# A hybrid HGRN and Hyena layer with a gated FFN on one core: half of the output projection under the spectral products, the other half token tile by token tile into the FFN

## What is computed

```python
def _mixer(h, rows, s0, l, p):
    proj = jnp.einsum('bld,de->ble', h, p['w_in'][l])          # 4096 columns
    q, ff, fb, iv, g, hy = jnp.split(proj, cuts, axis=-1)
    ...                                                        # HGRN: chunked scans, 4 heads of 128
    o = o * lax.rsqrt(jnp.mean(o * o, axis=-1, keepdims=True) + EPS)
    o_hg = o.reshape(B, L, HG_WIDTH) * jax.nn.silu(g.astype(F32))
    hyc = _dwconv3(hy, p['hy_conv_w'][l], rows).astype(F32)
    v, x1, x2 = jnp.split(hyc, [HY_WIDTH, 2 * HY_WIDTH], axis=-1)
    u = x1 * v
    z = _long_conv(u, kern) + p['hy_d'][l].astype(F32) * u
    y_hy = x2 * z
    y_hy = y_hy * lax.rsqrt(jnp.mean(y_hy * y_hy, axis=-1, keepdims=True) + EPS) * p['hy_norm_w'][l]
    merged = jnp.concatenate([o_hg, y_hy], axis=-1)
    return jnp.einsum('ble,ed->bld', merged, p['w_out'][l])

def _layer(x, cvec, rows, s0, l, p):
    ...
    x = x + g1 * mix
    h = _rmsnorm(x, p['norm2_w'][l]) * (1 + sc2) + sh2
    x = x + g2 * _convffn(h, rows, l, p)   # up 1024 -> 5632, conv, silu(gate) * val, down 2816 -> 1024
```

## Time and profile before

| what | value |
|---|---|
| median of 3 runs | 1025.52 us (1025.45 to 1026.12) |
| profiled execution, its own time | 1025.82 us |
| its span | 1024.0 us |
| busy share of the span | PE 92%, PE weight loads 81%, DVE 62%, ACT 32%, POOL 1% |
| chain that ended last | PE 81%, DVE 12%, ACT 3%, DMA 2% |
| mean granted clock of PE | 0.971 of full speed |

### The profile page before, as it was taken

How to read it: one execution, slowest core, us unless ns; L and a number is a source line. 1 busy time by engine, 2 the same in 40 slices (tenths; PEclk the granted TensorE clock), 3 DMA queues, 4 the chain that set the end, 5 groups by cost and what they waited for, 6 DMA issues and landing times.

```text
span 1024.0 us, 13691 instructions
## 1 busy us (share of the span) xinstructions
PE 944.6 (92%) x5564; PEld 825.9 (81%) x5564; DVE 639.3 (62%) x825; ACT 330.5 (32%) x571; POOL 14.6 (1%) x24
## 2 busy tenths in 40 slices
PE   6789999999999999549797999999999999999996
PEld 1247988989899889238676999988999998899985
DVE  4874357687586775886548666643666664466655
ACT  2462432342433422104116333321233331133332
POOL 0000000000000000000100000000000000000000
PEclk9899999999999999869997999999999999999998
DMA  8544234323432333021511222222122222222102
GB/s 298 189 166 162 79 127 144 89 83 124 149 117 67 111 125 98 0 103 41 185 42 62 83 83 72 74 83 83 62 83 71 74 81 86 74 71 70 55 1 103
DMA packets 26711, 99.06 MB, mean 97 GB/s; under 512 B 3256, under 2 KB 3640, under 8 KB 26009
## 3 DMA queue, kind: packets, MB, share of 16 engines
q1 hardware_dynamic: 24728, 89.06, 26.0%
q0 software_dynamic: 1920, 9.13, 2.7%
HBM read 95.01 MB, written 3.16 MB: 96 GB/s over the span
## 4 chain that ended last, share of the span: by engine, by line
PE 81%; DVE 12%; ACT 3%; DMA 2%; issue 2%; POOL 0%; SPq 0%; ACTq 0%; DVEq 0%
PE ps L1197 23%; PE ps L1199 22%; PE ps L1198 22%; PE ps L1375 3%; PE ps L1215 2%; DVE h_lo L817 1%; PE ps L1491 1%; PE ps L1234 1%; DMA x<-in_x_prompt 1%; DMA raw<-in_slots 1%; DVE h_hi L816 1%; PE ps L1387 1%; PE ps L1225 1%; PE ps L1464 1%; PE ps L1395 0%
## 5 line engine op out<-in xcount | busy, mean ns | idle before, releaser
L1197 PE MATMUL ps<-h_hi,w_hi 128*128 128x320 f32 x1152 | 360.4, 313 | 0.1
L1199 PE MATMUL ps<-h_hi,w_lo 128*128 128x320 f32 x1152 | 355.9, 309 | 0.0
L1198 PE MATMUL ps<-h_lo,w_hi 128*128 128x320 f32 x1152 | 355.8, 309 | 0.0
L1197 PEld LDWEIGHTS ps<-h_hi,w_hi 128*128 128x128 f32 x1152 | 216.4, 188 | 2.2 <-ACT KK L689 0.8
L1198 PEld LDWEIGHTS ps<-h_lo,w_hi 128*128 128x128 f32 x1152 | 216.4, 188 | 0.1
L1199 PEld LDWEIGHTS ps<-h_hi,w_lo 128*128 128x128 f32 x1152 | 216.2, 188 | 0.0
L809 DVE TENSOR_TENSOR w_lo<-raw,w_hi 128x1024 fp32r<-128x1024 f32 x106 | 129.3, 1225 | 128.4 <-ACT w_hi L548 123.7
L548 ACT ACTIVATE w_hi<-raw 128x1024 fp32r<-128x1024 f32 x106 | 111.1, 1052 | 134.4 <-PE ps L1199 126.2
L1197 PE MATMUL ps<-w_hi,a_hi 128*128 128x512 f32 x220 | 86.7, 394 | 0.0
L1199 PE MATMUL ps<-w_hi,a_lo 128*128 128x512 f32 x220 | 86.3, 392 | 0.0
L1198 PE MATMUL ps<-w_lo,a_hi 128*128 128x512 f32 x220 | 85.4, 388 | 0.0
(11 more groups left out here) (249 smaller groups left out, 1081.6 us busy)
## 6 DMA issues: line engine op xcount, KB each, us to landing
raw<-in_slots SPq DMA_DIRECT2D x154, 512.0 KB, 3.8
xin<-in_x_sample SPq DMA_DIRECT2D x4, 512.0 KB, 6.0
grow<-gates POOLq DMA_DIRECT2D x1, 2048.0 KB, 7.2
x<-in_x_sample POOLq DMA_DIRECT2D x4, 512.0 KB, 6.4
out_y_sample<-x SPq DMA_DIRECT2D x4, 512.0 KB, 2.6
decay<-in_decay SPq DMA_DIRECT2D x1, 1280.0 KB, 10.7
ktab<-in_ktab SPq DMA_DIRECT2D x1, 1024.0 KB, 5.8
utab<-in_utab POOLq DMA_DIRECT2D x1, 1024.0 KB, 6.3
```

The lines of the kernel that those rows point to most:

```text
L1197: mm(out, lhs[0], rhs[0], start=first, stop=False)
L1198: mm(out, lhs[0], rhs[1], start=False, stop=False)
L1199: return mm(out, lhs[1], rhs[0], start=False, stop=last)
```

## The change

1. In the projection the order of a head's tiles becomes q, ff, fb, Hyena, Hyena, g, the x2 tiles of Hyena come last, and the head steps begin with half 7 instead of 9. ACT's `ada_row` goes ahead of the wait for the half. The first three units of the output projection are split during the last tiles.
2. The heads' outputs are split between the two joins of the u spectrum. PE multiplies the HGRN half of the output projection (both column halves, 10 results) right after the forward transforms; ACT copies the results raw to `x1`.
3. The Hyena row norm no longer scales y ahead of the product: y times its weight is split per 128 channels as soon as it is there (`split_y`), the sums over channels are made token-major as five columns, and the reciprocal root of 128x5 scales the result rows in `mix_tile`, which also adds the HGRN half, the gate and the residual. The inverse tables use the memory of the forward ones, and residual rows and gates are loaded after the spectral products.
4. PE multiplies the second half tile by tile (`mix`), turns each tile (`turn_tile`) as soon as it is normed, and the FFN begins with the first halves of three up tiles, which need token tiles 0 to 2 only (`ffn_halves`); tiles 3 and 4 are turned between them.
5. The FFN's splits stand `LEAD_FFN` = 4 units ahead and behind the work of the unit, instead of 3 and ahead of it.

The diff's core:

```diff
-    for _kind in ("q", "hy", "ff", "fb", "hy", "g"):
+    TILES += [("q", _g), ("ff", _g), ("fb", _g), ("hy", HY_TILES[2 * _g]), ("hy", HY_TILES[2 * _g + 1]), ("g", _g)]
-FIRST_STEP = 9
+FIRST_STEP = 7
+LEAD_FFN = 4
+def ffn_halves(r):
+    units = range(2 * ROUNDS[r][1])
+    first = 3 if r == 0 else 0
+    return [(u, half) for half in range(2) for u in units[:first]] + [(u, half) for u in units[first:] for half in range(2)]
...
 # ACT, projection loop
                 for unit in ahead(n):
                     split_hi(unit)
+                if n in ADA_TURN:
+                    ada_row(ADA_TURN[n])
                 eng.wait_ge(sem("half_made"), n + 1)
...
-                if n in ADA_TURN:
-                    ada_row(ADA_TURN[n])
...
 # ACT, the HGRN half and the tiles
+            for n in range(2):
+                for i in range(NT):
+                    eng.wait_ge(sem("hg_mixed"), n * NT + i + 1)
+                    A(x1[:, n, i, :], ps[:, HG_BANKS[(n * NT + i) % 2], :], ACT.Copy).then_inc(sem("raw_taken"), 1)
+                for k in range(2):
+                    split_hi(UNIT_WOUT + 4 + 2 * n + k)
+            def scale_tile(i):
+                eng.wait_ge(sem("norm_used"), i + 1)
+                A(xn[:, i % 2, :].rearrange("p (n c) -> p n c", c=HW), x1[:, :, i, :], ACT.Copy,
+                  scale=stat[:, 1, 1, i:i + 1]).then_inc(sem("xn_ready"), 1)
+            def modulate_tile(i):
+                for k in range(KD):
+                    last = A(hf2[:, i % 2, k * P:(k + 1) * P], ps[:, TURN_BANKS[i] + k // 4, k % 4 * P:(k % 4 + 1) * P],
+                             ACT.Identity, scale=gain[:, 1, k, s:s + 1], bias=mod[:, 3 * KD + k, s:s + 1])
+            norm_tile(0)
+            scale_tile(0)
+            norm_tile(1)
+            scale_tile(1)
+            modulate_tile(0)
+            norm_tile(2)
+            scale_tile(2)
+            modulate_tile(1)
+            modulate_tile(2)
+            split_hi(UNIT_FFN)
+            norm_tile(3)
+            scale_tile(3)
+            split_hi(UNIT_FFN + 1)
+            modulate_tile(3)
+            norm_tile(4)
+            scale_tile(4)
+            split_hi(UNIT_FFN + 2)
+            modulate_tile(4)
+            split_hi(UNIT_FFN + 3)
...
 # DVE
+            join_u(0)
+            eng.wait_ge(sem("half_made"), NH)
+            link(V.tensor_copy(h_hi[:, 0:NC, :], o_hg[:, :, :]))
+            link(V.tensor_tensor(h_lo[:, 0:NC, :], o_hg[:, :, :], h_hi[:, 0:NC, :].bitcast(F32), ALU.subtract), "heads_split")
+            join_u(1)
+            split_lo(UNIT_WOUT + LEAD)
+            multiply(0)
+            multiply(1)
+            for k in range(2):
+                split_lo(UNIT_WOUT + 4 + k)
...
+            def mix_tile(i):
+                link(V.scalar_tensor_tensor(out=x, in0=ap(ps, MIX_BANKS[i] * 512, row), scalar=rhy[:, 2, i:i + 1],
+                                            in1=x, op0=ALU.mult, op1=ALU.add), "mixed_taken")
+                link(V.tensor_tensor(x, x, ap(grow1, s * D, row), ALU.mult))
+                link(V.tensor_tensor(x, x, ap(xres, i * D, row), ALU.add), "x1_ready")
+            def norm_row(i):
+                eng.wait_ge(sem("norm_ready"), NT + i + 1)
+                link(V.reciprocal(stat[:, 1, 1, i:i + 1], stat[:, 1, 1, i:i + 1]), "norm_used")
+            mix_tile(0)
+            norm_row(0)
+            mix_tile(1)
+            norm_row(1)
+            mix_tile(2)
+            split_tile(0)
+            norm_row(2)
+            mix_tile(3)
+            split_tile(1)
+            split_tile(2)
+            split_lo(UNIT_FFN)
+            norm_row(3)
+            mix_tile(4)
+            split_lo(UNIT_FFN + 1)
+            split_tile(3)
+            norm_row(4)
+            split_lo(UNIT_FFN + 2)
+            split_tile(4)
+            split_lo(UNIT_FFN + 3)
...
                 for n in range(2):
                     for k in range(nf // 2):
-                        split_lo(unit + LEAD)
+                        split_lo(unit + LEAD_FFN)
                         unit += 1
                     for i in range(NT):
                         eng.wait_ge(sem("down_made"), (2 * r + n) * NT + i + 1)
...
 # PE
+            for n in range(2):
+                units = [unit_ready(UNIT_WOUT + 2 * n + p) for p in range(2)]
+                for i in range(NT):
+                    ...
+                    last.then_inc(sem("hg_mixed"), 1)
...
+            mix(0)
+            mix(1)
+            mix(2)
+            turn_tile(0)
+            eng.wait_ge(sem("ysum_ready"), 1)
+            mix(3)
+            turn_tile(1)
+            turn_tile(2)
+            eng.wait_ge(sem("h_full"), KD + 1)
+            mix(4)
+            def before_half(n):
+                at = n - NH
+                if at >= 3:
+                    eng.wait_ge(sem("half_free"), n - 2)
+                if at in (0, 3):
+                    eng.wait_ge(sem("h_split"), KD + (3, 5)[at // 3])
+                if at == 1:
+                    turn_tile(3)
+                    eng.wait_ge(sem("mixed_taken"), 4)
+                if at == 2:
+                    turn_tile(4)
```

More of the change, by code:

```diff
@@ L171, in stream @@
                 out += [("ada", e, 2 * j), ("ada", e, 2 * j + 1)]
-    return out + [("weight", n) for n in range(UNIT_WOUT, NU)]
+    return out + [("weight", n) for n in range(UNIT_WOUT + LEAD, NU)]
 STREAM = stream()
@@ new lines, in _ @@
+                for u, half in ffn_halves(r):
+                    f, gv = divmod(u, 2)
+                    t = t0 + f
+                    eng.wait_ge(sem("half_made"), n + 1)
+                    if t >= 2 and half == 0:
+                        eng.wait_ge(sem("fconv"), 2 * (t - 2) + gv + 1)
+                    spread(ps[:, half_bank(n), 0:HT], padf[:, t % 2, gv, :], half, "half_free")
+                    n += 1
+                    if half and gv == 0:
+                        eng.wait_ge(sem("fconv"), 2 * t + 1)
+                        A(cf[:, 0, :], cf[:, 0, :], ACT.Silu).then_inc(sem("silu_done"), 1)
+                    elif half:
+                        eng.wait_ge(sem("act_ready"), t + 1)
+                        if r and f == 0:
+                            eng.wait_ge(sem("down_made"), 2 * r * NT)
+                        A(a_hi[:, f, :], actf[:, :], ACT.Copy).then_inc(sem("ahi_ready"), 1)
+                    if half:
+                        split_hi(unit + LEAD_FFN)
+                        unit += 1
@@ L1417, in half_product, with turn_u @@
                 last.then_inc(sem("half_made"), 1)
+            def turn_u(i):
+                for c in range(NC):
+                    if i < 4:
+                        e, k = divmod(i, 2)
+                        src = ap(u_hy, c * T + 2 * P * k + e, [(2, P)])
+                    else:
+                        src = u_hy[:, c, TS:T]
+                    last = nc.tensor.transpose(ps[:, U_BANKS[i], c * P:(c + 1) * P], src, ident[:, :])
+                last.then_inc(sem("u_turned"), 1)
             for n in range(NH):
@@ L1474, in sum_channels @@
             def sum_channels(c):
                 eng.wait_ge(sem("ysq_ready"), c + 1)
[L1476 to L1478 removed]
+                for i in range(NT):
+                    last = mm(ps[:, SUMS, c * NT + i:c * NT + i + 1], sq[:, i * P:(i + 1) * P], ones[:, 0:1],
+                              start=True, stop=True)
@@ L1517, in _, with mix @@
-            turn(xn, 1, (), lambda k: None)
+            units = [unit_ready(UNIT_WOUT + 4 + p) for p in range(4)]
+            def mix(i):
+                order = [(n, k) for k in range(NC, KD) for n in range(2)]
+                if i:
+                    order.sort()
+                for n, k in order:
+                    if i == 0 and n == 0:
+                        eng.wait_ge(sem("y_split"), k - NC + 1)
+                    last = split_product(ps[:, MIX_BANKS[i] + n, :], [x[:, k, i * P:(i + 1) * P] for x in (h_hi, h_lo)],
+                                         [w[:, k % 2 * HW:(k % 2 + 1) * HW] for w in units[2 * n + (k - NC) // 2]],
+                                         k == NC, k == KD - 1)
+                    if i == NT - 1 and k == KD - 1:
+                        last.then_inc(sem("wout_used"), 1)
+                    elif k == KD - 1 and n == 1:
+                        last.then_inc(sem("mixed"), 1)
+                    if i == 0 and k == KD - 1 and n == 0:
+                        sum_channels(NC - 1)
@@ L1528, in _ @@
+                unit += 2 * nf
                 for half in range(2):
```

515 lines of the change are left out of this document (249 added, 266 removed).

## The result

| | before | changed |
|---|---|---|
| median | 1025.82 us (1025.45 to 1028.58, 4 runs) | 992.90 us (990.59 to 994.55, 4 runs) |
| profiled execution | 1025.82 us, span 1024.0 | 991.46 us, span 989.7 |
| ratio | | 0.9672 (0.9642 to 0.9701) |
| busy share of PE, DVE, ACT | 92%, 62%, 32% | 95%, 64%, 35% |

The change is faster, but 992.9 us lies above the range of 974 to 992; of the 43.5 us forecast, 34.4 came between the two profiled executions and 32.9 between the medians. To find the missing 9.2 us I cut both profiled executions at four marks that PE's rows give: the first product of the projection, the end of the forward transforms (start plus duration of the last product with `ptab`), the first product of the first down half, and the end of the span.

The account below looks back on a forecast made before the run. PE's waits and half-speed clock between 401 and 557.5 us, chiefly for DVE's spectral products, were taken as the main loss. 1025.8 - 7.1 - 43.0 + 6.6 = 982.3, against the median 982 us, range 974 to 992.

Parts of the forecast that it names:

- part 1: Projection: copying the adaLN row ahead of the wait removes PE waits of 8.4 us; -7.1 us, bounds 0 to 8.4.
- 4 x 1.0 + 2 x 1.2 + 2 x 0.3: Projection: the us gained from the eight adaLN row waits, giving 7.0, taken as 7.1.
- Rival (b): Projection: DVE becomes the bound, convolution delays QQ, the row copy gives nothing or loses; about 989 us, chance 0.12.
- part 2: Transforms to inverse transform: products end 3.2 us later, HGRN half fills PE, 2.8 us idle, full-speed start saves 2.6 us.
- A gap of 2.8 us is shorter than 4, so the inverse transform starts at full speed: Ahead of the inverse transform: PE's clock falls only 4 us after stopping, so it stays full; saves 2.6 us.
- part 4: Output projection into FFN, tile by tile: fourth FFN half starts at 525.1 instead of 568.1 us; -43.0 us.
- The mark of the kernel before: FFN start: first product taken at 557.54 us, so the fourth half at 557.54 + 10.55 = 568.1 us.
- rival (a): Tile stage: PE's clock falls, 1.5 to 2.6 us each; with down gaps 987 to 992 us, chance 0.14.
- the hand-made chain of some 25 links: Tile stage: DVE and ACT steps from 479.85 us, walked through to the fourth half's start at 525.1.
- part 5: FFN down halves: fourth split ahead of the add stalls PE about 3 us in two rounds; +6.6 us, bounds 0 to 9.6.

Follow-up runs that it names:

- e4: Kernel before with only the adaLN row copy moved ahead of the wait for the half; 1024.08 us, ratio 0.9951.
- e7: Changed kernel with the adaLN row copy put back behind the half's bank; 995.01 us, ratio 0.9677.
- e5: Changed kernel run again as a control, nothing edited; 993.88 us, ratio 0.9654, profiled execution 986.63 us.
- e1: Changed kernel with the fourth weight split of each down half put behind the five adds; 982.76 us, ratio 0.9555.
- e8: Changed kernel without the three first halves taken ahead: the FFN begins only when tile 4 is split; 1001.00 us, ratio 0.9739.
- e3: Changed kernel with constant products on PE in five waits, ahead of the inverse transform and in the tile stage; 989.32 us, ratio 0.9623.
- e10: Changed kernel with the edits of e1 and e2 alone, no constant products; 980.70 us, ratio 0.9543.
- e2: Changed kernel with two weight splits moved from ahead of the context's product to behind it; 989.97 us, ratio 0.9625.
- e6: Changed kernel with the edits of e1 and e2 plus constant products in the four waits of the tile stage; 976.85 us, ratio 0.9508.
- e9: Kernel of e6 with six more constant products in a PE wait of the start-up, ahead of the second adaLN turn; 978.39 us, ratio 0.9509.

## Why the prediction was wrong

**Projection (part 1): right, and undersized.** The row copy gives 6.5 us by itself (e4 forwards, e7 backwards) where 7.1 was forecast; the sum 4 x 1.0 + 2 x 1.2 + 2 x 0.3 counts 1.2 us for two waits of at most 1.1, and with 1.05 it gives 6.7. The whole stretch gave 8.8. The other 2.3 us come with the rest of the first point of the change (order of tiles, steps two halves earlier), which the prediction priced at nothing: PE's waits from 100 us to the end of the transforms add up to 5.8 us in e4 and to 3.5 in the changed kernel, where the largest is 0.9 instead of 1.92 and the 0.57 us ahead of the transforms are gone. No run separates the order of tiles from the earlier steps. Rival (b) fell: no wait for QQ or kc exceeds 0.9 us.

**Spectral products and the HGRN half (part 2): the plan held, one step failed.** From the end of the transforms to the inverse transform it took 30.1 us, with 2.89 us of waiting. The prediction's 30.0 and 2.8 match by a slip: it puts the end of the transforms at 423.2, but 422.77 + 1.02 is 423.79, and from there its own marks give 29.4 us and a wait of 2.2. So 0.7 us of the shortfall lies here. The failed step is "A gap of 2.8 us is shorter than 4, so the inverse transform starts at full speed". From one long gap, behind whose start the clock fell after 4 us, I made a threshold. The same wait was followed by a fall in three profiles (the first, e5, e7) and by none in two (e1, e8).

**Tile by tile (part 4): two steps failed.** The mark of the kernel before was one half too late, since the timeline was read where a duration of 0.42 us looked like a beginning: 3.4 us. And rival (a) was set aside with the argument that no wait is above 2.8 us; it happened, with three falls counting the one of part 2, and by e3 against the first profile they cost 5.6 us. What is left of the 10.2 us is 1.2: the 0.7 us above, and 0.5 us in the hand-made chain of some 25 links, which from the inverse transform to the first FFN product takes 56.29 us in e1, where no fall delays it, and was forecast at 55.75. The chain was otherwise good: passes from PSUM of 1.28 us (forecast 1.24), and the two waits that differ in the first profile are, where the clock stays full around them, 0.54 us (forecast 0.65) and 1.64 us (1.5), in e5.

**Down halves (part 5): right.** The split at 654.12 ahead of the add, 3.16 us of wait, two rounds. From the first down product to the next round's first up product it takes 54.95 us before and 58.15 in e5: 3.2 us a round, 3.3 forecast. Against e1 (54.43) a stall costs 3.7 us, and where the clock falls behind it 1.3 more (59.45 in the first profile).

**Sum.** 982.3 + 3.4 (mark) + 5.6 (clock in the third stretch) + 1.2 (end of the transforms and chain) + 0.7 (last stretch: + 1.3 for the clock behind one stall, - 0.2 for the two stalls, - 0.4 in the last round) - 1.7 (projection) = 991.5 us, the profiled execution. The 1.7 us of the projection were luck: without them the miss would have been larger. The median of 992.9 lies 1.4 higher. I put that down to the start-up and the clock, which both vary between executions, but unprofiled runs don't show where.

The prediction cited the Trainium skill ("TensorE: Matmul & The Clock Gate", section "HAM oscillation — how this bites in real kernels"), by which short pieces of matmul with waits between them let the clock drop again. What it left out is that the waits in that section's example are 3 to 5 us. The traces here show falls behind shorter ones too, from 2.4 us on, but not at every piece. The same page ("What's actually happening") says that what the hardware watches does not restart with the kernel, so that the point at which one kernel changes speed varies from run to run. The first profile and e5 are the same program and agree: the clock falls behind the wait at 503 us in the one and not in the other.

**What stays open.** Of the twelve profiled executions three had a start-up of 79.0 to 79.4 us (before, changed, e5) and nine one of 82.1 to 82.4. Four filter products take 1.98 us in the one (35.34 us in the first profile) (2.40 in e5) and 3.78 in the other, so PE's clock, read from these durations, is part of it. Whether the changed kernel meets the longer one more often than the kernel before was not tested.

## What to carry to other kernels

Price each new wait of PE of 1 to 3 us with a stretch of slow clock as a chance, not as a yes or no by its length, and where executions scatter by more than an edit is worth, compare stretches between two marks of the trace. Where a split, copy or load is moved one buffer further ahead, look for the first thing queued behind it that frees a bank: here one split put behind the adds took 7.4 us (against e5) to 8.7 us (against the first profile) out of the fourth stretch, and with two more edits it made a kernel of 976.9 us, faster than both. Take a mark such as "the first product of a stage" from the row where the operands change, and count instructions to the next mark: 32 halves of 3.52 us back from 667.2 would have given 554.6 and not 557.5.

## What the runs showed of the hardware

- The granted clock fell behind waits of 2.4 to 3.2 us (and in e10 behind two of 1.6 and 1.3 us with 1.1 us of work between) in some executions and not in others, with the same wait and the same instructions around it: the wait of 2.9 us ahead of the inverse transform had a fall behind it in three profiles of five, and that of 2.7 us ahead of the third tile's turn in e1, e5, e7 and e10, but not in the first profile, e2 and e8. In e5 PE already worked for 0.6 us when it fell, so the fall need not come within the wait.
- With constant products into an unused bank in its waits, the granted clock was 1.00 from 440 to 530 us in all three profiles that have them (128x512 and 128x256 in e3, 128x256 in e6 and e9), and fell at least once there in the seven without. They delayed nothing that the profile shows: the inverse transform starts 30.06 us behind the transforms in e3 and 30.14 in the first profile.
- A fall whose slow work ends in a wait for another engine is nearly free (494 us in e5: the wait behind it shrinks from 2.42 to 1.11 us); others cost about half their busy time or somewhat less (1.5 us for 2.97 us at the inverse transform, 1.3 us for 3.30 behind a down wait).
- The granted clock in the rows can disagree with the durations: from 35 to 45 us e9 reads 1.00 and e6 0.50, with 3.78 us for the same four filter products in both.
